# Reordering two kinds of adding transfers on the Pool queue, and one low part at the entry of the FFN, in a two-layer decoder trunk

## What is computed

```python
for layer in range(DEPTH):                     # DEPTH = 2
    xn = rms_norm(h, norm_mix_g[layer])
    ...                                        # mixer: pooling + differential attention, or conv + block attention
    h = h + mix
    hn = rms_norm(h, norm_ffn_g[layer])
    h = h + (silu(hn @ ffn_w_gate[layer]) * (hn @ ffn_w_up[layer])) @ ffn_w_down[layer]
return rms_norm(h, norm_final_g)
```

## Time and profile before

| | |
|---|---|
| median of 3 runs | 558.1 us (558.05 to 558.82) |
| time of the profiled execution | 559.87 us |
| its span, first to last instruction | 558.0 us |
| granted TensorE clock, mean share of full | 0.999 |
| PE, weight load, DVE, ACT, Pool busy | 98%, 83%, 85%, 63%, 5% |
| moved by DMA | 122.42 MB, 219 GB/s over the span |

### The profile page before, as it was taken

The page is one execution under the profiler, slowest core; times in us unless marked ns, Lnnn a source line. Parts: engine busy times, 40 slices in busy tenths (PEclk is TensorE's granted clock), DMA queues, the critical chain, the costliest instruction groups (busy, mean ns, idle before and its releaser), DMA issues.

```text
span 558.0 us, 7380 instructions
## 1 busy us (share of the span) xinstructions
PE 548.7 (98%) x2805; PEld 461.0 (83%) x2805; DVE 474.1 (85%) x564; ACT 348.9 (63%) x475; POOL 29.0 (5%) x70
## 2 busy tenths in 40 slices
PE   8999999999999999999999999999999999999996
PEld 7899978887888788888888888888788888878785
DVE  5769996798989999878798998977989898989765
ACT  6877664664767486655666366646576666748524
POOL 1200001100000010000000000001010000000000
PEclk9999999999999999999999999999999999999999
DMA  8995546845979879774469422409789697977102
GB/s 295 409 404 196 189 150 211 270 123 132 298 258 286 307 203 340 189 286 167 151 256 346 174 76 76 151 29 292 284 221 339 187 314 243 295 284 211 56 0 75
DMA packets 32867, 122.42 MB, mean 219 GB/s; under 512 B 3648, under 2 KB 4800, under 8 KB 30784
## 3 DMA queue, kind: packets, MB, share of 16 engines
q1 hardware_dynamic: 30384, 105.04, 49.8%
q0 software_dynamic: 2304, 16.78, 15.7%
q10 hardware_dynamic: 144, 0.14, 0.1%
HBM read 120.89 MB, written 1.05 MB: 219 GB/s over the span
## 4 chain that ended last, share of the span: by engine, by line
PE 71%; DVE 16%; DMA 5%; issue 4%; ACT 3%; POOL 0%; SPq 0%; DVEq 0%; ACTq 0%; POOLq 0%
PE bank L1792 12%; PE bank L1794 12%; PE bank L1793 12%; DVE w_lo L1133 7%; PE bank L2266 5%; PE bank L2265 5%; PE bank L2270 5%; PE bank L1903 4%; PE bank L2237 3%; DMA spare<-in_slabs 2%; DMA sixth_raw<-in_slabs 2%; PE bank L1906 2%; DVE raw L1597 2%; PE bank L2242 1%; ACT w_hi L682 1%
## 5 line engine op out<-in xcount | busy, mean ns | idle before, releaser
L1133 DVE TENSOR_TENSOR w_lo<-raw,w_hi 128x2048 fp32r<-128x2048 f32 (+2 forms) x71 | 156.2, 2211 | 21.5 <-ACT w_hi L682 21.0
L682 ACT ACTIVATE w_hi<-raw 128x2048 fp32r<-128x2048 f32 (+2 forms) x66 | 120.8, 1846 | 5.0 <-DMA raw<-in_slabs 2.8
L1792 PE MATMUL bank<-w_lo,yT_hi 128*128 128x512 f32 (+1 forms) x226 | 91.3, 404 | 2.2 <-DVE yT_lo L1690 1.6
L1794 PE MATMUL bank<-w_hi,yT_lo 128*128 128x512 f32 (+1 forms) x226 | 88.1, 390 | 0.0
L1793 PE MATMUL bank<-w_hi,yT_hi 128*128 128x512 f32 (+1 forms) x226 | 87.8, 389 | 0.0
L1133 DVE TENSOR_TENSOR w_lo<-sixth_raw,w_hi 128x2048 fp32r<-128x2048 f32 x22 | 50.3, 2285 | 5.0 <-ACT w_hi L682 5.0
L1792 PEld LDWEIGHTS bank<-w_lo,yT_hi 128*128 128x128 f32 x226 | 42.5, 188 | 13.1 <-DVE yT_lo L1690 4.2
L2265 PE MATMUL bank<-w_hi,forms_hi 128*128 128x512 f32 x128 | 50.4, 394 | 0.0
L1794 PEld LDWEIGHTS bank<-w_hi,yT_lo 128*128 128x128 f32 x226 | 42.4, 188 | 9.1
L2266 PE MATMUL bank<-w_hi,forms_lo 128*128 128x512 f32 x128 | 49.9, 390 | 0.0
L1793 PEld LDWEIGHTS bank<-w_hi,yT_hi 128*128 128x128 f32 x226 | 42.6, 189 | 7.4
(11 more groups left out here) (289 smaller groups left out, 1136.5 us busy)
## 6 DMA issues: line engine op xcount, KB each, us to landing
raw<-in_slabs SPq DMA_DIRECT2D x146, 512.0 KB, 7.7
sixth_raw<-in_slabs SPq DMA_DIRECT2D x28, 512.0 KB, 7.6
sixth_raw<-in_slabs POOLq DMA_DIRECT2D x6, 1024.0 KB, 11.3
spare<-in_slabs SPq DMA_DIRECT2D x12, 512.0 KB, 4.9
raw<-in_slabs POOLq DMA_DIRECT2D x6, 1024.0 KB, 8.8
spare<-in_slabs POOLq DMA_DIRECT2D x4, 1024.0 KB, 10.4
raw<-in_slabs SPq DMA_DIRECT2D x5, 256.0 KB, 4.6
h<-in_x SPq DMA_DIRECT2D x2, 512.0 KB, 6.7
```

Of the source, the lines that this page charges most:

```text
L682: A(w_of(s, c), raw_of(r, c), ACT.Copy).then_inc(hi_ready, 1)
L1133: V.tensor_tensor(w_of(s, c, 1), raw_of(preps[s][0], c), w_of(s, c).bitcast(F32), ALU.subtract).then_inc(lo_ready, 1)
L1792: T.matmul(o, st_hi, mv_lo, start=first, stop=False, skip_group_check=onto)
L1794: return T.matmul(o, st_lo, mv_hi, start=False, stop=last, skip_group_check=onto)
```

## The change

- Pool issues, per layer, T3(2), T3(4), T4(2), T3(6), T4(4), T3(8), T4(6), T4(8), in place of T3(2), T4(2), T3(4), T4(4), T3(6), T4(6), T3(8), T4(8). No transfer is added or dropped, and each keeps its own waits.
- The T3 transfers alternate between two semaphores, so that the counts of neighbouring ones do not mix.
- At the entry, DVE does `activate(3, 1)` and `at_lo_evac(2, 0, 0, 1)` first and the low part of T3(2), f + 6, after them. The same instructions run.

```diff
-        third_added = sem("third_added")
+        third_added = [sem(f"third_added{i}") for i in range(2)]
...
+        def third_sum(l, a):
+
+            n = seven_no(l, a)
+            return third_added[n % 2], 16 * (n // 2) + 16
+
...
-                sum_of_prep[place["t3", l, a]] = (third_added, 16 * seven_no(l, a) + 16)
+                sum_of_prep[place["t3", l, a]] = third_sum(l, a)
...
                 if (kind, a, b) in (("norm", 1, 1), ("norm", 3, 1)):
-                    for unit in SEVEN_AT[a // 2]:
-                        add_third(a // 2, unit)
-                        add_fourth(a // 2, unit)
+                    l, units = a // 2, SEVEN_AT[a // 2]
+                    add_third(l, units[0])
+                    for unit, following in zip(units, units[1:]):
+                        add_third(l, following)
+                        add_fourth(l, unit)
+                    add_fourth(l, units[-1])
...
-                        dve.wait_ge(third_added, 16 * seven_no(l, a) + 16)
+                        dve.wait_ge(*third_sum(l, a))
...
                 block_add(SEVEN_AT[l][0], 0)
-                split_los(f + 6)
                 activate(3, 1)
                 at_lo_evac(2, 0, 0, 1)
+                split_los(f + 6)
                 split_forms()
```

More of the change, by code:

```diff
@@ L638, in add_third @@
                 pool.wait_ge(raw_loaded[y], made)
-                nc.gpsimd.dma_start(raw_of(y), piece(n, 0, SLAB), accum_op=ALU.add).then_inc(third_added, 16)
+                nc.gpsimd.dma_start(raw_of(y), piece(n, 0, SLAB), accum_op=ALU.add)\
+                    .then_inc(third_sum(l, a)[0], 16)
             def add_fourth(l, a):
```

## The result

The changed kernel takes 563.88 us (median of 8 runs, 560.49 to 565.72), the kernel before beside it 558.78 (8 runs, 558.05 to 560.47). The ratio is 1.0075, with a 95% interval of 1.0043 to 1.0108: slower by three quarters of a per cent, and outside the range of 556.0 to 561.2. The profiled execution took 565.49 us with a span of 563.7, against 559.87 and 558.0 of before.

| | before | after |
|---|---|---|
| time of the profiled execution | 559.87 us | 565.49 us |
| its span | 558.0 us | 563.7 us |
| granted TensorE clock, mean | 0.999 | 0.993 |
| moved by DMA | 219 GB/s | 217 GB/s |

A forecast was written before the change was run, and what follows sets the result against it. PE, busy for 98% of the span, was taken to bound the kernel. Layer 0 at -0.6 and layer 1 at +1.2 (+2.5 - 1.3) gave +0.6 us, 558.1 to 558.7 us, with a range of 556.0 to 561.2.

The forecast's parts named there:

- The four stalls: PE's FFN stalls at both layers' entries, at 189.35 and at 495.89 go: 2.73 us at most.
- layer 0: First FFN: stalls of 0.95 us go, part lost to T4(4): -0.6 us, from -0.95 to +0.4.
- T4(4) of layer 0: Queued behind T3(6), 0 to 1 us late; even on time only 0.15 of the entry's gain is kept.
- What T3(4) takes from the loads: Layer 0: without T3(4) among the loads, home y of unit 6 lands about 5 us earlier, at 155.5.
- The -1.29 of unit 8: Layer 1: the PE stall at 495.89 goes since T3 lands far earlier than needed: -1.29 us.
- T3(4) of layer 1: Issued at about 402.4 once its home is loaded, takes 9.0 us, lands at 411.4.
- The price of T4(2): Layer 1: issued at 411.65 behind T3(4), takes 9.5 us, the dearest T4, and lands at 421.15.
- the first rival: All four stalls go without T4 being late: 558.1 - 2.7 = 555.4, between 555.4 and 557; chance 0.22.
- Who waits: For a late T4: ACT's high part, then DVE's low part, then all that follows on DVE.
- DVE's chain: Layer 1, unit 2: low part at 423.1, DVE 3.3 us late, slack 0.78, so PE leaves 2.5 us later.
- T4 becomes the late one: Layer 1: T4(2) lands at 423 to 425.5, PE 4.4 to 6.8 us late: 560.6 to 563.0; chance 0.24.
- The cover holds: Layer 1's T3(4) and T4(2) take some 8 us each, or T4(2) isn't held: 555.4 to 557; chance 0.22.

The follow-up runs named there:

- e1: The kernel before with only the entry's edit (T3's low part done after the other two), Pool's order as before: 558.11 us against 558.94, ratio 0.9979.
- e3: The changed kernel with Pool's new order in the first FFN only, the entry's edit in both layers: 557.6 us against 558.94, ratio 0.9972.
- e4: The changed kernel with 832 bytes in place of 512 for the descriptors of Pool's transfers: 560.05 us against 558.94, ratio 1.0007.
- e2: The changed kernel with the entry as before, so Pool's new order alone: 562.1 us against 558.94, ratio 1.0063.
- e6: The changed kernel with layer 1's loads behind T4(2) held until T4(2) has landed: 566.13 us against 558.4, ratio 1.0133.
- e7: The changed kernel with 20 more thrown-away matmuls on PE ahead of its wait before `b22`, layer 1, unit 2: 561.45 us against 558.4, ratio 1.0089.
- e8: The changed kernel with 832 bytes for descriptors and layer 1's loads held until T4(2) has landed: 557.07 us against 558.4, ratio 0.9979.
- e9: The kernel before with the entry's edit and 832 bytes for descriptors, Pool's order left alone: 556.73 us against 558.4, ratio 0.9969.
- e11: The changed kernel once more as it is, twelve runs for the spread of its times: 563.91 us against 558.51, ratio 1.0083.
- e5: The kernel before with 832 bytes for the descriptors and nothing else: 557.95 us against 558.51, ratio 0.9986.

## Why the prediction was wrong, point by point

**The four stalls.** Right in all four places, and in layer 0 about right in size: 0.6 forecast, 0.77 measured in the profiled execution; the seven other traces with both edits there have 1.2 to 1.4. T4(4) of layer 0 was issued at 165.41, 1.2 us behind the block addition that it waits for, where it had been 0.7 behind: some 0.5 late (forecast 0 to 1). Its high part began at 174.98 against 174.65. The product behind it started at 186.04 against 185.80, which in a run that had begun 0.46 later is 0.22 of the entry's 0.49 kept, where I had 0.15. What T3(4) takes from the loads was put too high: without it home y of unit 6 was full 4 us earlier (at about 156.7, less the run's later start, against 160.7), not 5. The 152 GB/s "alone" of the earlier trace rows are not quite that, since loads were issued from 137.57 on, within that window. The -1.29 of unit 8 was in the profiled run, though e1's and e3's traces show that stall at 0.2 to 0.5; on the median I had counted it too high.

**T3(4) of layer 1.** Right: issued at 402.38 (402.4), landed at 410.8 (411.4). T4(2) was issued at 411.08 (411.65), held until the other had landed. This step, Pool's wait and its reason, was right, and e4 shows the reason.

**The price of T4(2).** This is the first term that failed. I took 9.5, the dearest T4, and had up to 11.5 as a bound; 12.7 lies above that and even, by 0.1, above the dearest T3 of the earlier trace rows. With a landing of 423.78, the prediction's own steps give DVE's low part at 425.74 (425.75 in the trace), 5.9 late, and PE 5.2 late in place of 2.5. The prediction had three loads "from about 412 on" and the transfer at 411.65 in its text, and under the first rival it said that every T3 that met loads within about a us took 11.1 or more. The sum still priced T4(2) by the T4s, which had all been issued 2.4 us and more ahead of the next load. With T4(2) itself the nearness made the price: 0.24 to 0.43 us ahead of the load 12.4 to 12.8, 0.98 ahead 10.5, 3.2 ahead 8.3.

The Trainium skill, "DMA: Bandwidth & Descriptors", section "Queues, rings and completion order", says that each engine takes turns between its queues, packet by packet. By that a lead of a few tenths of a us should matter little. The T3s among several loads agree, 11.2 to 12.6 in no order of their lead; T4(2) does not, with 2.2 us between a lead of 0.3 and one of 0.98. The runs don't separate where that arises.

**Who waits.** I followed DVE's list from T4's low part on. ACT's list was nearer: T4's high part, a down slab's, the copy of T1's result, and `b22` behind it. For a landing of 421.15 this chain would have put `b22` at 421.15 + (428.05 - 423.78) = 425.4, 1.8 behind the 423.64 of before. That is less than the 2.5 of DVE's chain, so the omission cost the sum nothing. It did hide that the wait would be one piece ahead of `b22`, long enough for the clock.

**The clock.** This is the second term that failed, since the sum put it at nothing: a stall of 5.3 us left PE at 1.2 GHz for the 12 matmuls of `b22`, 2.57 us more. After stalls of 2.1 to 2.2 us in the same place (e2, e4) the matmuls were at full clock; after 4.9 us in e6 they were not. e7, with PE kept at work through the wait, has them at full clock. The Trainium skill, "TensorE: Matmul & The Clock Gate", section "HAM oscillation — how this bites in real kernels", has this as a trap: waits for DMA between bursts of matmuls make the next burst start at the lower clock. The trace agrees, 0.50 granted from 428 to 432.

**In sum.** Forecast +0.6, measured +5.7 in the profiled pair and 4.2 by the ratio of the runs. In layer 1's own time `b22` of unit 2 began 4.67 us late (428.05 against 423.64, and 0.26 for the earlier start) where the forecast had PE 2.5 late. So of the 5.1 between forecast and profile 2.17 is the dear T4(2), 2.57 the clock, and 0.46 the later start of the profiled run's first FFN, which the change has no part in; layer 0 took 0.12 off. The rival "T4 becomes the late one" named this mechanism, with landings of 423 to 425.5, and its own price was 560.6 to 563.0 since it, too, left out the clock. The stated range held only 0.6 of the 2.4 us of that rival's times; the text's "about a third" left out should have been three quarters. I gave it 0.24 on the ground that one load only stood beside T3(4); that was true of T3(4) and didn't bear on T4(2). "The cover holds" fell for layer 1. The Trainium skill's price that spoke for it ("DMA: Bandwidth & Descriptors", section "Anatomy of one DMA", 4.4 us as an estimate) is under six tenths of the least that any trace here shows, 7.6.

**Open.** Why so small a lead decides, whether by the order in which descriptors are fetched or by what is queued in the 16 engines, was not taken apart. e4's T4(2) took 12.5 us though issued 3.2 us ahead of its nearest load behind (410.3), but T3(4) and the load of 402.5 were still in flight then; with the next loads held as well (e8) it took 9.8. So a lead over the next load is not all of it, and the T3s say the same. The spread of the changed kernel's single times, 558 to 568 over both sets, has no trace to explain it.

## What to carry to other kernels

When a transfer is moved on a queue, price the one that now stands behind it: its issue time, the distance to the next load, and how many loads follow. If several loads follow within a us or two, take the price from transfers that had such neighbours, and not from those that had quiet. A second transfer that waits on "issue" for the first to land may only lack room for its descriptors, and then a larger reserve with the old order can gain what the new order was to gain, without its cost (e9). A PE stall that grows to about 5 us should be counted with matmuls at half clock behind it, here 12 of them for 2.6 us.

## What the runs showed of the hardware

- One adding transfer of 1 MB took about 8 us in quiet (7.6 at the least). A T4 with four loads of 1 MB issued from 0.02 to 0.43 us behind it on took 12.4 to 12.8 (changed kernel, e6, e7, e11); T3s issued among several loads took 11.2 to 12.6. In the changed kernel half of the next load landed 5.3 us after its issue, long before the adding transfer ahead of it.
- With a reserve of 512 a second adding transfer went out 0.26 us behind the landing of the first; with 832 it went out 0.54 us behind the issue of the first, and then took 14.6 to 15.3 (e5, e9) where it had taken 11.3 to 12.6.
- The granted clock was 0.50 behind standstills of PE of 4.9 and 5.3 us and 1.00 behind those of 2.1 and 2.2.
- An edit that gains by itself (e1, 0.9979) went with a larger loss elsewhere: with it T4(2) took 12.7, without it 10.5, in one trace of each. By the totals the two kernels are not apart, 1.0075 and 1.0083 against 1.0063, with intervals that overlap.
